# Decode attention on one Trainium2 core: the order in which POOL issues the value block and the key block of a step

## What is computed

```python
def fox_sample(q, k_new, v_new, log_f_new, cache_k, cache_v, cache_logf, page_table):
    B, T = q.shape[:2]
    past_k = cache_k[page_table].reshape(B, -1, H_FOX, HEAD_DIM)
    past_v = cache_v[page_table].reshape(B, -1, H_FOX, HEAD_DIM)
...
    return fox_attend(q, k_all, v_all, g_new, bias_k, q_pos, k_pos)

def fox_attend(q, k, v, bias_q, bias_k, q_pos, k_pos):
    s = jnp.einsum('bqhd,bshd->bhqs', q, k).astype(jnp.float32) * ATTN_SCALE
    s = s + jnp.transpose(bias_q, (0, 2, 1))[:, :, :, None] + jnp.transpose(bias_k, (0, 2, 1))[:, :, None, :]
...
    p = jax.nn.softmax(s, axis=-1)
    return jnp.einsum('bhqs,bshd->bqhd', p.astype(v.dtype), v)
```

## Time and profile before

| | us |
|---|---|
| median of three executions | 2654.69 |
| lowest and highest | 2649.76, 2660.79 |
| the profiled execution | 2660.36 |
| its span in the profile | 2658.8 |
| PE busy | 2419.8 |
| POOL busy | 407.6 |
| key blocks: first and last load issued | 680.0, 1326.0 |
| value blocks: first and last load issued | 757.6, 1372.6 |

### The profile page before, as it was taken

The page is one execution under the profiler, slowest core; times in us unless marked ns, Lnnn a source line. Parts: engine busy times, 40 slices in busy tenths (PEclk is TensorE's granted clock), DMA queues, the critical chain, the costliest instruction groups (busy, mean ns, idle before and its releaser), DMA issues.

```text
span 2658.8 us, 45752 instructions
## 1 busy us (share of the span) xinstructions
PE 2419.8 (91%) x18509; PEld 2196.5 (83%) x18509; DVE 1024.8 (39%) x1351; ACT 860.2 (32%) x994; POOL 407.6 (15%) x833
## 2 busy tenths in 40 slices
PE   6699988999789998999979894999999999899996
PEld 4699988999666666666649892999999999899995
DVE  1344333343333333333316435333343334344444
ACT  2122322333233332333322223343433433333322
POOL 2001000000133333333321000111111111122210
PEclk8699999999899999999989997999999999899998
DMA  6145434454589999999985642576767767588881
GB/s 185 40 142 172 147 98 128 140 163 130 170 285 342 336 358 325 352 319 337 358 278 181 197 138 97 176 242 236 236 230 240 246 218 238 179 269 272 285 269 60
DMA packets 338550, 585.65 MB, mean 220 GB/s; under 512 B 20067, under 2 KB 282491, under 8 KB 334415
## 3 DMA queue, kind: packets, MB, share of 16 engines
q0 software_dynamic: 70288, 308.92, 33.3%
q1 hardware_dynamic: 268128, 274.86, 32.9%
HBM read 564.01 MB, written 109.34 MB: 253 GB/s over the span
## 4 chain that ended last, share of the span: by engine, by line
PE 78%; DMA 9%; DVE 6%; ACT 3%; issue 3%; POOL 1%; POOLq 0%; SPq 0%; DVEq 0%; ACTq 0%
PE ps L726 14%; PE ps L727 13%; PE ps L728 13%; DMA kraw<-in_cache_fox_k 6%; PE ps L792 6%; PE ps L794 6%; PE ps L793 6%; PE ps L929 3%; PE ps L934 2%; PE ps L954 2%; DMA kraw<-in_cache_win_k 2%; PE ps L735 1%; ACT w_hi L1132 1%; PE ps L1014 1%; DVE w_lo L1405 1%
## 5 line engine op out<-in xcount | busy, mean ns | idle before, releaser
L1405 DVE TENSOR_TENSOR w_lo<-raw,w_hi 128x2048 fp32r<-128x2048 f32 (+2 forms) x252 | 528.8, 2099 | 998.2 <-ACT w_hi L1132 998.1
L1132 ACT ACTIVATE w_hi<-raw 128x2048 fp32r<-128x2048 f32 (+2 forms) x252 | 442.9, 1758 | 913.5 <-PE ps L728 641.1
L726 PE MATMUL ps<-act_hi,w_hi 128*128 128x320 f32 x1664 | 515.8, 310 | 29.4 <-DVE act_lo L1434 22.5
L727 PE MATMUL ps<-act_lo,w_hi 128*128 128x320 f32 x1664 | 515.4, 310 | 0.0
L728 PE MATMUL ps<-act_hi,w_lo 128*128 128x320 f32 x1664 | 515.3, 310 | 0.0
L792 PE MATMUL ps<-act_hi,w_hi 128*128 128x320 f32 x1088 | 344.2, 316 | 0.0
L726 PEld LDWEIGHTS ps<-act_hi,w_hi 128*128 128x128 f32 x1664 | 313.5, 188 | 30.1 <-issue 30.1
L794 PE MATMUL ps<-act_hi,w_lo 128*128 128x320 f32 x1088 | 337.6, 310 | 0.0
L793 PE MATMUL ps<-act_lo,w_hi 128*128 128x320 f32 x1088 | 337.5, 310 | 0.0
L727 PEld LDWEIGHTS ps<-act_lo,w_hi 128*128 128x128 f32 x1664 | 313.6, 188 | 0.0
L728 PEld LDWEIGHTS ps<-act_hi,w_lo 128*128 128x128 f32 x1664 | 313.5, 188 | 0.0
(11 more groups left out here) (324 smaller groups left out, 3704.9 us busy)
## 6 DMA issues: line engine op xcount, KB each, us to landing
raw<-in_w_gate_up SPq DMA_DIRECT2D x88, 1024.0 KB, 7.2
kraw<-in_cache_fox_k POOLq DMA_DIRECT2D x128, 512.0 KB, 6.8
vraw<-in_cache_fox_v POOLq DMA_DIRECT2D x128, 512.0 KB, 7.3
raw<-in_w_in SPq DMA_DIRECT2D x60, 1024.0 KB, 7.8
raw<-in_w_gate SPq DMA_DIRECT2D x32, 1024.0 KB, 14.3
raw<-in_w_down SPq DMA_DIRECT2D x32, 1024.0 KB, 6.1
out_win_k_sample<-in_cache_win_k POOLq DMA_DIRECT2D x64, 510.0 KB, 5.8
out_win_v_sample<-in_cache_win_v POOLq DMA_DIRECT2D x64, 510.0 KB, 4.1
```

The lines of the kernel that those rows point to most:

```text
L726: pe.matmul(ps[:, bk_, 0:T], w_hi[:, slot, k, :], xh[:, x_k, :], start=(k == k0), stop=False)
L727: pe.matmul(ps[:, bk_, 0:T], w_hi[:, slot, k, :], xl[:, x_k, :], start=False, stop=False)
L1132: act.activation(w_hi[:, slot, 0:kt, :], raw[:, pslot, 0:kt, P * slot:P * slot + P], ACT.Copy).then_inc(hi_done, 1)
L1405: dve.tensor_tensor(w_lo[:, slot, 0:kt, :], raw[:, pslot, 0:kt, P * half:P * half + P], w_hi[:, slot, 0:kt, :].bitcast(F32), ALU.subtract) ...
```

## The change

In every step POOL issues the value block first and the key block second. The small loads keep their place behind "their" block: the bias behind key block 1, the new values behind value block 6.

```diff
             def load_blocks(kb, vb):
                 for n in range(KPG):
+                    if vb is not None:
+                        load_values(vb, n)
+                        if n == 6:
+                            load_new_values(vb)
                     if kb is not None:
                         load_keys(kb, n)
                         if n == 1:
                             load_bias(kb)
-                    if vb is not None:
-                        load_values(vb, n)
-                        if n == 6:
-                            load_new_values(vb)
 
             load_blocks(0, None)
             for b in range(1, DB):
```

## The result

| | before | with the change |
|---|---|---|
| median, ten runs each | 2654.28 us | 2668.19 us |
| lowest and highest | 2649.76, 2661.16 | 2663.82, 2675.25 |
| the profiled execution | 2660.36 | 2666.15 |
| its span | 2658.8 | 2664.6 |

The ratio is 1.0049, 95% interval 1.0037 to 1.0062: the change makes the kernel 13.9 us slower, by the ratio close to the 0.5% that the chances were drawn at. The time lies in the stated range of 2639 to 2682. It lies 1 us above the narrower range of 2648 to 2667 that the balanced case was given, and the size isn't that of the forecast: 2.1 us were forecast. The two profiled executions differ by 5.8 us only, since that of before was one of its slower ones. So the profiles show where time goes, and the medians how much.

What follows compares the result with a forecast made beforehand. Seven rounds were taken as close to full on both PE and DMA. Only 0.3 us per round for step 2 counted, other terms 0: 7 x 0.3 = 2.1 us, giving 2657 us, range 2639 to 2682.

Steps and rivals of the forecast that it cites:

- the balanced case: Whole kernel: the change stays within 0.5% (13 us) of no change, own range 2648 to 2667 us; chance 60%.
- the slower case: Whole kernel: slower by a block per series of key waits or part of it, beyond 13 us; chance 23%.
- What bounds the kernel: Seven rounds, 572 us: PE and DMA both close to full; load order can shift at most 76.7 us of waits.
- When POOL can issue: Each step's block loads: key issue moves by +0.19 us, value issue by -2.18 us; 0 in the sum.
- Round start: Steps 1 and 2: V1's 4.07 us wait turns into a longer wait for K2; gain 0, cost 0 to 1.31 us.
- What stands ahead of a key: DMA queue: one more value block ahead of each key, 0 to 1.31 us per series of key waits; taken as 0.
- Step 2: Long step 2 of a round: the queue gets its second block 3.3 us later; cost taken as 0.3 us per round.
- New values: Two small loads, now between V6 and K6: K6 some 1.3 us late; hidden, taken as 0.
- The signs: Changed trace: value waits under 5 us, key waits 70 to 80, key landing up 0.5 to 1.3, rounds within 1 of 82.
- The last sign: PE: the prediction would also be wrong if a longer single wait lowered the granted clock behind it; no size given.
- if the sum of both waits grows by more than 15 us: Key plus value waits, 76.7 us before: such growth means four value buffers didn't carry the extra block; prediction wrong, slow side.
- The slower rival: Round start and two further series: each series of key waits begins one block later, 27.5 us, 2682 us; chance 23%.

Runs made afterwards that it cites:

- experiment 8: Four kernels: page numbers and new values early, key first 2654.05 us, value first 2666.09; each key's page number loaded twice, key first 2663.94, value first 2675.89.

## Why the prediction was right in sign and wrong in size

The forecast of 2.1 us was below the 13 us that the measurement was said to tell from no change, so the sign is no great hit. By the prediction's own split, 13.9 us belong to the slower case, to which it gave 23%; by the ratio of 1.0049 they end just within the balanced one. That the time lies in the stated range owes more to the width of that range than to the sum.

**What bounds the kernel: right.** PE had the same instructions and the DMA the same bytes, and in the two profiles the change stayed mostly in waits for blocks. The order cost little, 0.5%.

**When POOL can issue: right.** V starts 0.68 us behind the products (1048.38 to 1049.06) and K 0.87 us behind its transposes (1049.41 to 1050.28), 0.17 us later than before, where the prediction had worked out 0.19 us (and put it at 0 in the sum, as hidden):

```profile
1047.77 0.61 PE L1014 MATMUL ps<-vraw,pt 128*16 128x256 f32 x8
1048.81 0.60 PE L934 MATMUL ps<-ident,kraw 128*128 128x128 f32 x4
1049.06 0.53 POOL L632 DMA_DIRECT2D vraw<-in_cache_fox_v  x1 [1.72 <-PE ps L1014]
...
1050.28 0.53 POOL L625 DMA_DIRECT2D kraw<-in_cache_fox_k  x1 [0.69 <-issue]
```

**Round start: right.** V1's wait of 4.07 us went and K2's grew from 1.23 to 5.72 us (the forecast said 4 to 6). From the bias to K2 it took 1020.89 - 1003.65 = 17.24 us before and 1022.25 - 1004.57 = 17.68 after, 0.44 us, between the bounds of 0 and 1.31, of which the sum had taken 0:

```profile
1016.40 0.13 PEld L1014 LDWEIGHTS ps<-vraw,pt 128*16 128x16 f32 x8 [0.19 <-issue]
1022.25 0.71 PEld L929 LDWEIGHTS ps<-ident,kraw 128*128 128x128 f32 x4 [5.72 <-DMA kraw<-in_cache_fox_k]
```

**What stands ahead of a key: taken too low.** The step that failed is the choice of 0, "the first key that PE waits for then lands where it landed". The runs show otherwise: PE's idle time for keys went from 23.1 to 49.3 us while 20.1 us for values went away, and the order costs 10 to 14 us at each of three amounts of work on POOL. That is 1.4 to 2.0 us per round, inside the term's own bounds of 0 to 3 x 1.31 us, and I took the end of them and not a value between. No run shows how many blocks a key had before it, so that the extra block was only partly paid back is argued from the price.

**Step 2: the spacing right, the cost open.** Forecast 3.3 us between K5 and V6 beyond the old spacing, and 0.3 us of cost "as 6.9 us of room were free anyway". The spacing came (4.93 against 1.15 us). The stretch with room moved less, 0.4 us of transfer in the round shown when the windows are set to the start of the round, near the 0.3 us of the sum; with unshifted windows it would be 1.2 us. No experiment sets this term apart: the nearest one, three value buffers, shows 4.3 us in seven rounds, which isn't clear of the noise of two profiles.

**New values: no more than part.** Forecast hidden. Moving them gave back 0.2% when they alone were moved, and nothing beyond the early page loads (1.0028 against 1.0025) when both were. They cost POOL time behind the products, and experiment 8 shows that POOL's time counts.

**The signs.** Waits for fox values vanished as forecast, key waits reached 75.2 us (forecast 70 to 80). The median landing of keys didn't rise (7.1 to 7.0 us, forecast 0.5 to 1.3 more), so this was no measure of what a waiting key suffers. The rounds took 83.4 us from bias to bias where they had taken 82.3 (forecast: within 1 us of 82), at the share of 0.97 that was forecast. The last sign, a lower clock behind a longer single wait, did come in one round, see below. And the test "if the sum of both waits grows by more than 15 us" was put on a view that couldn't show it: 76.7 and 75.2 us by weight loads, 43.2 and 49.3 us by products.

**The slower rival**, one block per series of key waits, had the direction and twice the measured price: 27.5 us against 13.9. Its mechanism isn't shown. How the 10 to 14 us of the order divide between the key's place in the queue, the later issue of the value block in long steps and PE's clock stays open: no kernel changed one of them with the others and the number of buffers kept.

## What to carry to other kernels

Where two streams share one queue and the consumer takes A before B in each step, try A first, both issued as soon as A's buffer is free, even if B's buffer would be free earlier. In this kernel the other order cost 0.5%, and 1.6% where B wasn't let out ahead of the wait for A's buffer. Set windows to the start of the round before they are compared: a shift of 1 us made 0.4 us look like 1.2. And before a suspect is convicted by taking it away, take it away on the other side too: the early page loads looked like half of the loss until they were run with the old order.

## What the runs showed of the hardware

After a long single wait PE ran at a lower granted clock. In the round at 1087 us before, K2 came after two waits of 0.88 and 1.15 us and the waits that followed were of 1.7 us at most; the clock stayed 1.00. With the change there were waits of 2.55 and 3.36 us in their place (1104.60 and 1122.72 us), and the same round, bias to bias, first before, then after, reads:

```profile
1087.54:1167.42 79.88, 74.00 (x829) 52.78 (x825) 28.76 (x64) 28.58 (x50) 27.75 (x53) 1.00 0.99 343
```

```profile
1090.09:1174.29 84.20, 77.75 (x826) 56.06 (x826) 28.69 (x64) 28.65 (x50) 27.70 (x53) 0.94 0.96 326
```

The round is 4.32 us longer, and PE is busy for 3.75 us more with as many products, at 0.94 of the clock. Right behind the second wait the granted clock is 0.50, the lower of its two levels (1.2 GHz):

```profile
1122.00:1125.00 3.00, 2.27 (x10) 2.27 (x11) 0.27 (x1) 0.60 (x1) 0.00 (x0) 0.50 1.03 410
```

Four weight loads of a key took 0.69 and 0.71 us behind the two long waits, and 0.42 us behind a short one:

```profile
1101.50 0.42 PEld L929 LDWEIGHTS ps<-ident,kraw 128*128 128x128 f32 x4 [1.15 <-DMA kraw<-in_cache_fox_k]
```

```profile
1104.60 0.69 PEld L929 LDWEIGHTS ps<-ident,kraw 128*128 128x128 f32 x4 [2.55 <-DMA kraw<-in_cache_fox_k]
...
1122.72 0.71 PEld L929 LDWEIGHTS ps<-ident,kraw 128*128 128x128 f32 x4 [3.36 <-DMA kraw<-in_cache_fox_k]
```

By a rule of the Trainium skill ("TensorE: Matmul & The Clock Gate", section "What's actually happening") PE falls from 2.4 to 1.2 GHz when it has been idle. The trace agrees, with the 0.50 above.

What this costs in all is open. Over the seven rounds of the two profiles it is small: other rounds made up for this one, and PE's busy time grew by 1.1 us. But the mean granted clock of an execution was 0.9545 over the ten runs with the change, and 0.957 over the runs of the kernel before beside the experiments. With two levels, 1.00 and 0.50, that is some 13 us more at the lower one, in which PE loses half of the time that it is busy: up to some 7 us of the 13.9, an estimate. So the clock may be a good part of what the order costs, and no experiment separates it. That one long wait costs more than the same time in two short ones is what the round at 1087 us suggests, and no run tested it alone.

A second load of a page number by POOL, a few instructions per key, cost 0.26% with the key first. I had expected its wait for the transposes to hide it, on an engine that is busy for 15% of the span.
